# Delta-rule stage of a two-block kernel: direction 1 keeps its states in the other row half, and the read-out uses four quarters and two banks by row half

## What is computed

```python
def rwkv7_scan(r, w, k, v, kk, a, reverse):
    def step(state, inp):
        r_t, w_t, k_t, v_t, kk_t, a_t = inp
        sa = jnp.einsum('bhij,bhj->bhi', state, -kk_t)
        state = (state * w_t[:, :, None, :] + sa[..., None] * (kk_t * a_t)[:, :, None, :]
                 + v_t[..., None] * k_t[:, :, None, :])
        return state, jnp.einsum('bhij,bhj->bhi', state, r_t)
    ...
y = (rwkv7_scan(r_h, decay[:, :, 0], k_dir[:, :, 0], v_h, kk, a[:, :, 0], False)
     + rwkv7_scan(r_h, decay[:, :, 1], k_dir[:, :, 1], v_h, kk, a[:, :, 1], True))
```

## Time and profile before

| | us |
|---|---|
| median of 3 runs | 1690.05 (1689.94 to 1690.85) |
| profiled execution, its own time | 1690.36 |
| its span, first to last instruction | 1688.6 |
| TensorE busy | 1648.6 (98%) |
| VectorE busy | 1063.7 (63%) |
| ScalarE busy | 725.0 (43%) |

### The profile page before, as it was taken

One profiled execution on the slowest core, in us unless ns is written; L12 is line 12 of the kernel. 1 busy time (PEld: TensorE's weight loads), 2 busy tenths in 40 slices (PEclk: granted clock), 3 DMA queues, 4 the chain that ended last, 5 costly groups with the idle time before them and its releaser, 6 DMA issues. The chain is left out here.

```text
span 1688.6 us, 30303 instructions
## 1 busy us (share of the span) xinstructions
PE 1648.6 (98%) x12924; PEld 1299.4 (77%) x12924; DVE 1063.7 (63%) x1517; ACT 725.0 (43%) x1092; POOL 98.9 (6%) x123
## 2 busy tenths in 40 slices
PE   9999999999999999999999999999899999999997
PEld 6666767778767888888888788884477878888887
DVE  6867588878667577576765762446885654343434
ACT  5444555544264443232314454237664543232323
POOL 0000000000000100001111000030100000000001
PEclk9999999999999999999999999999999999999999
DMA  6212221112145344446562232320002232332331
GB/s 226 82 63 69 100 90 41 41 41 97 35 169 180 127 160 150 151 162 223 192 220 83 84 101 70 124 77 1 1 2 76 87 101 100 100 100 88 102 98 50
DMA packets 50500, 171.56 MB, mean 102 GB/s; under 512 B 5824, under 2 KB 9152, under 8 KB 49600
## 3 DMA queue, kind: packets, MB, share of 16 engines
q1 hardware_dynamic: 40640, 133.46, 23.1%
q0 software_dynamic: 9728, 36.18, 6.4%
HBM read 160.71 MB, written 8.39 MB: 100 GB/s over the span
## 5 line engine op out<-in xcount | busy, mean ns | idle before, releaser
L373 PE MATMUL pair<-h_hi,w_hi 128*128 128x512 f32 x1008 | 401.7, 398 | 2.8 <-DVE w_lo L419 2.2
L375 PE MATMUL pair<-h_hi,w_lo 128*128 128x512 f32 x1008 | 392.8, 390 | 0.0
L374 PE MATMUL pair<-h_lo,w_hi 128*128 128x512 f32 x1008 | 392.6, 390 | 0.0
L419 DVE TENSOR_TENSOR w_lo<-w_raw,w_hi 128x1024 fp32r<-128x1024 f32 (+2 forms) x225 | 266.5, 1186 | 156.1 <-ACT w_hi L398 155.9
L398 ACT CAST w_hi<-w_raw 128x1024 fp32r<-128x1024 f32 (+2 forms) x225 | 222.2, 990 | 218.4 <-PE pair L375 215.4
L373 PEld LDWEIGHTS pair<-h_hi,w_hi 128*128 128x128 f32 x1008 | 189.2, 188 | 57.9 <-issue 17.5
L374 PEld LDWEIGHTS pair<-h_lo,w_hi 128*128 128x128 f32 x1008 | 189.4, 188 | 39.9 <-issue 2.6
L375 PEld LDWEIGHTS pair<-h_hi,w_lo 128*128 128x128 f32 x1008 | 189.3, 188 | 39.8
L373 PE MATMUL pair<-ff_f_hi,w_hi 128*128 128x512 f32 (+1 forms) x536 | 204.1, 381 | 0.6 <-DVE w_lo L419 0.6
L375 PE MATMUL pair<-ff_f_hi,w_lo 128*128 128x512 f32 (+1 forms) x536 | 203.5, 380 | 0.0
L374 PE MATMUL pair<-ff_f_lo,w_hi 128*128 128x512 f32 (+1 forms) x536 | 203.5, 380 | 0.0
(11 more groups left out here) (453 smaller groups left out, 2483.4 us busy)
## 6 DMA issues: line engine op xcount, KB each, us to landing
w_raw<-in_w_ff SPq DMA_DIRECT2D x128, 512.0 KB, 3.3
mod_w<-in_w_mod POOLq DMA_DIRECT2D x48, 512.0 KB, 3.7
w_raw<-in_w_in SPq DMA_DIRECT2D x22, 512.0 KB, 3.3
w_raw<-in_w_gate SPq DMA_DIRECT2D x16, 512.0 KB, 3.3
w_raw<-in_w_out SPq DMA_DIRECT2D x16, 512.0 KB, 3.3
w_raw<-in_w_rwkv SPq DMA_DIRECT2D x15, 512.0 KB, 3.3
w_raw<-in_w_da SPq DMA_DIRECT2D x12, 512.0 KB, 4.7
w_raw<-in_w_ple_gate SPq DMA_DIRECT2D x8, 512.0 KB, 3.3
```

The costliest lines, as they stand in the source:

```text
L373: nc.tensor.matmul(out, w_hi, x_hi, start=(k == 0), stop=False)
L374: nc.tensor.matmul(out, w_hi, x_lo, start=False, stop=False)
L375: last = nc.tensor.matmul(out, w_lo, x_hi, start=False, stop=(k == kt - 1))
L419: nc.vector.tensor_tensor(lo[:, s % SPLIT_SLOTS, 0:cols], pr.raw[:, w % RAW_SLOTS, 0:cols], hi[:, s % SPLIT_SLOTS, 0:cols].bitcast(F32), A ...
```

## The change

Direction 1 keeps head hh in row half 1 - hh in all that reads a state: the output of the products for `Phi` and `psi` goes to `rows64(hh ^ d)`, and so the states `Z` lie there. What is multiplied with a state must lie in the same rows. For that `Rb` of direction 1 is written across halves, in two VectorE instructions of 64 partitions instead of one of 128, and the decays at chunk ends are copied across into a new small tile `ends` (two copies of 64x8 for each pair). In the last product a matmul now reads row half `hh ^ d` and writes partition half `hh`, and it goes to `bank[1 - half]`, a bank for each row half that is read. Hence y is the sum of both banks: ScalarE copies bank 0 (512 columns, semaphore `yhalf`), VectorE adds bank 1 to it and only then `yo` is raised.

```diff
-                        pe.wait_ge(s["yo"], 2 * p)
+                        pe.wait_ge(s["yo"], p)
...
-                                nc.tensor.matmul(out[h, at:at + 64], a["N"][rows64(cc), q, 64:128], a["BhN"][rows64(cc), b, h],
+                                nc.tensor.matmul(out[there, at:at + 64], a["N"][rows64(cc), q, 64:128], a["BhN"][rows64(cc), b, h],
...
-                    for b in range(TB):
-                        for cc in range(2):
-                            for d, a in both(p):
-                                for hh in range(2):
-                                    last = nc.tensor.matmul(pr.bank[1 - cc][rows64(hh), 64 * b:64 * b + 64],
-                                                            a["Z"][rows64(hh), 2 * b + cc, :],
-                                                            a["Rb"][rows64(hh), (2 * b + cc) * CH:(2 * b + cc + 1) * CH],
-                                                            start=False, stop=(d == 1), skip_group_check=True)
+                    for n in range(NCH):
+                        tokens = slice(CH * n, CH * n + CH)
+                        for d, a in both(p):
+                            for hh in range(2):
+                                half = hh ^ d
+                                last = nc.tensor.matmul(pr.bank[1 - half][rows64(hh), tokens], a["Z"][rows64(half), n, :],
+                                                        a["Rb"][rows64(half), tokens], start=False, stop=True, skip_group_check=True)
...
-                    for cc in range(2):
-                        nc.scalar.copy(U[:, p, :].rearrange("p (b cc t) -> p b cc t", b=TB, cc=2)[:, :, cc, :],
-                                       pr.bank[1 - cc][:, 0:256].rearrange("p (b t) -> p b t", b=TB)).then_inc(s["yo"], 1)
+                    nc.scalar.copy(U[:, p, :], pr.bank[0]).then_inc(s["yhalf"], 1)
...
+                def ends_across(p):
+                    a = dirs[1][p % 2]
+                    for h in range(2):
+                        nc.vector.tensor_copy(a["ends"][rows64(1 - h), :], a["pin"][rows64(h), :, 0]).then_inc(s["ends"], 1)
...
+                                if d == 0:
+                                    nc.vector.tensor_tensor(out, r, more, ALU.add).then_inc(s["rbout"], 1)
+                                else:
+                                    nc.vector.tensor_tensor(out[64:128], r[0:64], more[0:64], ALU.add)
+                                    nc.vector.tensor_tensor(out[0:64], r[64:128], more[64:128], ALU.add).then_inc(s["rbout"], 1)
+                    dve.wait_ge(s["yhalf"], p + 1)
+                    nc.vector.tensor_tensor(U[:, p, :], U[:, p, :], pr.bank[1], ALU.add).then_inc(s["yo"], 1)
                     gates.dve(dve, point + 20)
                     if p + 1 < RT:
                         masked(p + 1, 1)
```

More of the change, by code:

```diff
@@ L1116, in rwkv_block @@
                 Phi=R[:, :, 0:64], Z=E, BhN=td("bhn", [P, TB, P]), KhN=td("khn", [P, TB, P]))
-            dirs.append([dict(fixed, pin=pin[:, j], Rt=rkb[:, j, 0, :], Kt=rkb[:, j, 1, :], Bh=rkb[:, j, 2, :], RK=rkb[:, j, 0:2, :],
+            ends = td("ends", [P, 2, NCH]) if d else None
+            dirs.append([dict(fixed, pin=pin[:, j], ends=ends[:, j] if d else None, Rt=rkb[:, j, 0, :], Kt=rkb[:, j, 1, :], Bh=rkb[:, j, 2, :], RK=rkb[:, j, 0:2, :],
                               Kh=kh[:, j, :], Rb=kh[:, j, :], N=rkb[:, j, 1:3, :].rearrange("p a (q t) -> p (a q) t", t=P))
@@ L1128, in rwkv_block @@
                  "y5", "y64", "mv", "mvout", "n", "nout", "pp", "phiout", "psiout",
-                 "rb", "rbout", "step", "zout", "fixed", "y", "yo", "ksum", "bonus", "bsum", "bout", "scaled", "zero")
+                 "rb", "rbout", "ends", "yhalf", "step", "zout", "fixed", "y", "yo", "ksum", "bonus", "bsum", "bout", "scaled", "zero")
         s = pr.stage_sems("rw_", names)
@@ L1139, in chunks, with decay_ends @@
             return x.rearrange("p (n t) -> p n t", n=NCH)
+        def decay_ends(a, d, cols):
+            return a["ends"][:, cols].unsqueeze(2) if d else a["pin"][:, cols, CH:CH + 1]
         def heads_of(pair, first):
@@ L1379, in _ @@
                                 for hh in range(2):
-                                    q, h = hh * TB + b, rows64(hh)
+                                    q, h, there = hh * TB + b, rows64(hh), rows64(hh ^ d)
                                     for cc in range(2):
@@ L1383, in _ @@
                                         left, right = ((a["KhN"][r, b, h], vN[r, b, h]), (a["BhN"][r, b, h], a["N"][r, q, 0:64]))[part]
-                                        last = nc.tensor.matmul(out[h, at:at + 64], left, right, start=(part == 0), stop=(part == 1))
+                                        last = nc.tensor.matmul(out[there, at:at + 64], left, right, start=(part == 0), stop=(part == 1))
                         last.then_inc(s["pp"], 1)
@@ L1415, in _ @@
                                 left, right = ((vN[r, b, h], a["A2"]), (a["N"][r, q, 0:64], a["A1"]))[k]
-                                last = nc.tensor.matmul(pr.bank[1 - cc][h, 64 * b:64 * b + 64], left, right[r, q, :],
+                                at = CH * (2 * b + cc)
+                                last = nc.tensor.matmul(pr.bank[1 - cc][h, at:at + CH], left, right[r, q, :],
                                                         start=(b == 0 and d == 0 and k == 0), stop=False, skip_group_check=True)
@@ L1746, in _ @@
                         dve.wait_ge(s["pp"], 2 * p + d + 1)
+                        if d:
+                            dve.wait_ge(s["ends"], 2 * p + 2)
                         nc.vector.memset(a["Z"][:, ORDER[d][0], :], 0.0).then_inc(s["zero"], 1)
@@ L1757, in _ @@
                             slots = a["Z"][:, 2 * lo_b + cc + step:2 * (hi_b - 1) + cc + step + 1:2, :]
[L1758 removed]
+                            ends = decay_ends(a, d, slice(2 * lo_b + cc, 2 * (hi_b - 1) + cc + 1, 2))
                             psi = halves[:, cc, 256:512].rearrange("p (b t) -> p b t", b=TB)
@@ L1786, in _ @@
                             for d, a in both(p):
-                                nc.vector.tensor_tensor(a["Rb"].rearrange(order, b=TB, cc=2), a["Rt"].rearrange(order, b=TB, cc=2),
-                                                        heads_of(pr.pair[3], 256 * d), ALU.add).then_inc(s["rbout"], 1)
+                                out, r, more = (x.rearrange(order, b=TB, cc=2) if i < 2 else heads_of(pr.pair[3], 256 * d)
+                                                for i, x in enumerate((a["Rb"], a["Rt"], None)))
+                                if d == 0:
[5 more added lines that the diff above has]
+                    nc.vector.tensor_tensor(U[:, p, :], U[:, p, :], pr.bank[1], ALU.add).then_inc(s["yo"], 1)
                     gates.dve(dve, point + 20)
```

6 lines of the change are left out of this document (4 added, 2 removed).

## The result

| | us |
|---|---|
| before, median of 8 runs | 1690.41 (1689.78 to 1691.17) |
| after, median of 8 runs | 1695.35 (1694.49 to 1696.04) |
| ratio after to before | 1.0030, 95% interval 1.0021 to 1.0039 |
| profiled execution after, its own time | 1696.04 (span 1694.3) |

The account below looks back on a forecast made before the run. TensorE, busy 98% of the span, was taken to bound the kernel. Three times 0.87 + 0.48, plus 0.1, minus 0.28, made +3.87 us on the median of 1690.05: 1693.9 us, range 1692.0 to 1695.6.

Parts of the forecast that it names:

- the range's upper end: 1695.6 us: each boundary 0.3 us dearer for five handovers, and 0.7 us for small copies in one pair without cover.
- The last product: At each pair's end: on four quarters it takes 1.16 us in place of 2.05, 0.89 us less.
- The boundary, +0.87: Between pairs, three times: L1316 waits for copy, addition and first factors; 0.87 us later each, product's gain included.
- `Rb`, +0.48: Ahead of the next pair's transposes, three times: direction 1's two half-row instructions delay them, 0.48 us each.
- The rival of 0.60 us apart: VectorE's half instructions run close together: `Rb` costs 0.30, pair 3 nothing, +3.2 us in all, 1693.3; chance 0.18.
- Pair 3, +0.1: At step 2 of pair 3, without transposes to cover VectorE: a wait of some 0.1 us.
- The end of the stage, -0.28: Behind pair 3: product 0.92 us shorter, 1.34 us behind it in place of 0.70, so 0.28 us less.
- `ends_across` at nothing: Two 64x8 copies per pair on VectorE behind `scaled`: at most 0.7 us for both, covered by 1.6 us, costing nothing.

Follow-up runs that it names:

- kernel 1: The kernel before with only the last product put on four quarters and a bank for each row half (y wrong): 1687.08 us against 1690.08.
- Kernels 4 and 5: 4: changed kernel, addition moved behind next pair's masks, 1689.83 us; 5: changed kernel, ScalarE copies both banks in pairs 0 to 2, addition behind first factors, 1688.94 us.
- kernel 3: Changed kernel with `Rb` in one 128-partition instruction again, plus two-half split replaced by one unused 64-row instruction on the same rows (y wrong): 1694.24 us, ratio 1.0025.
- Kernel 7: Changed kernel with only the gate's pick-up moved ahead of VectorE's wait for ScalarE's copy: 1694.24 us against 1690.29.
- kernel 8: Kernel 5 with the transposes' banks in order 2, 6, 7, 6, 7, 2, so the second transposes wait for `Rb`: 1688.35 us against 1690.29.

## Why the prediction was right

The direction, the mechanism and the place of most of the loss were right, and the time was inside the range, 1.45 us above the forecast. That it was inside is in part luck: the range's upper end made room for dearer handovers at each boundary and for copies without cover, neither of which came, and the time used that room for an end of the stage whose sign was wrong and for dearer `Rb` steps. Of the 1.45 us, 0.36 are the base itself: the forecast started from 1690.05, and eight runs of the kernel before gave 1690.41.

- **The last product: right.** 1.11 to 1.16 us in all four pairs; alone it gains 3.0 us (kernel 1). The step is -0.93 us, 0.04 more than was taken.
- **The boundary, +0.87: right**, at +0.85 in each of three. The chain is the one that was written down: the copy starts 0.08 us behind the product (forecast 0.03), takes 0.59, VectorE starts 0.03 later, and L1675 0.60 behind the addition. Kernels 4 and 5 show the cause: with two of the four instructions ahead of the addition 1.45 us come back at each boundary, with all four ahead of it 1.78 us, and TensorE's wait in L1320 is gone. TensorE waited 1.56 us there, where some 1.7 were forecast.
- **`Rb`, +0.48: right in kind, 0.09 us too small, three times.** From the start of L1801 to the end of L1804 the trace has 2.09 us (344.92 to 347.01) where 2.06 was worked out, and TensorE starts 0.15 us behind that end (347.16) where 0.05 was taken from another place. The rival of 0.60 us apart is what kernel 3 shows for instructions on the same rows, and is wrong for these. What was said for it, that all VectorE instructions of this shape stand 0.60 us apart, misread the timeline: the first factors of the earlier trace rows have the same shape and stand 0.73 apart (355.70 to 357.88 for three of them).
- **Pair 3, +0.1:** +0.17 at step 2, for the same reason.
- **The end of the stage, -0.28: the term that was mis-sized**, +0.37 measured. The sum counted copy and addition behind the product (1.34 us; 1.38 was measured) and took the addition to be VectorE's last work. It left out what is queued behind it: `gates.dve(point + 20)` has one pick-up in pair 3, 0.59 us. Kernel 7 moves it, and 0.60 us come back; the end is then 0.23 us better than before (-0.92 + 0.69), near the forecast's 0.28.
- **`ends_across` at nothing: right**; each copy takes 0.17 us, half of the 0.35 that was the upper bound, and at `Phi` and `psi` the view of waits has TensorE waiting for none of VectorE's work.

These corrections turn 3.87 into 4.80 us. The other 0.9 us between the two profiled executions are gaps that no forecast named: 0.84 us up to 10 us from the program's start, where the code is the same, 0.66 us of gaps in the four pairs, 0.14 us of small steps, and 0.76 us given back behind the stage. They move without the change. At the start the eight other kernels, with the same code there, stand 0.2 to 1.4 us behind the kernel before. Kernel 7 has the changed kernel's TensorE instructions and lacks the gap of 0.55 us in pair 0 and the one of 0.35 us in pair 3. What makes them is open.

The gain of the product can be kept: kernel 8 computes what the changed kernel does and is 1.9 us faster than before (1688.35; by the interval 0.5 to 3.6), 7.0 us under the changed kernel by their medians.

## What to carry to other kernels

When one engine takes over a step that waits for another's result, look at every instruction behind it in that engine's stream, to the end of the block: here a wait of 1.5 us and the addition behind it, in front of four instructions that needed nothing from them, cost 1.78 us where the faster product gave 0.93. Put such an instruction behind all that does not need it, or let the engine that is idle anyway free the bank. And a wait that is removed is worth only the distance to the next one, so read that before moving it.

## What the runs showed of the hardware

- VectorE instructions of 512 columns that last 0.68 us and do not wait for one another start 0.60 us apart when they keep to the same rows, whether they have 128 rows or 64 (0.60, 0.60, 0.59), and 0.70 apart when they read one half and write the other. The instruction behind such a one, on all 128 rows, is held too (0.72). Where each has a semaphore wait for the one before, as the first factors have, they stand 0.72 to 0.73 apart on the same rows (361.12, 361.84, 362.57, 363.29).
- The last product's matmuls, which are added onto PSUM, run on four quarters as fast as the fresh sums of L1254: 64 records in 1.11 to 1.16 us (half of these matmuls meet a sum that L1416 left at their place), the two row halves writing the same partitions of two banks. Of 36 such products in nine kernels three took longer, 1.25 to 1.41 us (kernels 3 and 8).
- TensorE's stream has gaps of 0.2 to 1.3 us in this stage that the profile puts down to issue. They move between kernels whose TensorE instructions are the same, and sum to 0.9 to 1.9 us (1.2 before, 1.9 with the change, 1.2 in kernel 7).
